# A norm in halves at both ends of a two-layer encoder kernel, and its buffers moved to multiples of 512 bytes

## The reference, cut to what matters

```python
def rmsnorm(x, g):
    y = x * lax.rsqrt(jnp.mean(x * x, axis=-1, keepdims=True) + EPS)
    return y * g

def reference(...):
    for l in range(DEPTH):                    # DEPTH = 2
        hn = rmsnorm(h, mix_pre[l])
        mix = rglru_mixer(hn, ...)  if l == 0 else  swa_sink_attention(hn, ...)
        h = h + rmsnorm(mix, mix_post[l])
        f = swiglu(rmsnorm(h, ffn_pre[l]), ffn_w_gu[l], ffn_w_down[l])
        h = h + rmsnorm(f, ffn_post[l])
    return h
```

## Time and profile before

| | |
|---|---|
| runs, us | 1172.42, 1173.07, 1174.63 (median 1173.07) |
| profiled execution, us | 1173.57; span from the first to the last instruction 1171.6 |
| PE, matmul | 1140.4 us busy, 97% |
| DVE, ACT, POOL | 550.7 (47%), 451.9 (39%), 89.6 us (8%) |
| DMA | 106.98 MB, mean 91 GB/s |
| mean granted TensorE clock | 0.996 |

### The profile page before, as it was taken

How to read it: one execution, slowest core, us unless ns; L and a number is a source line. 1 busy time by engine, 2 the same in 40 slices (tenths; PEclk the granted TensorE clock), 3 DMA queues, 4 the chain that set the end, 5 groups by cost and what they waited for, 6 DMA issues and landing times.

```text
span 1171.6 us, 13468 instructions
## 1 busy us (share of the span) xinstructions
PE 1140.4 (97%) x5605; PEld 950.9 (81%) x5605; DVE 550.7 (47%) x688; ACT 451.9 (39%) x715; POOL 89.6 (8%) x73
## 2 busy tenths in 40 slices
PE   7999998999999999999999899999999999999997
PEld 6888887889888888888888878788888888888885
DVE  4868977756333333322237577446433333332224
ACT  5365565445223222221116467545323232221112
POOL 1003213200000000000012332100000000000000
PEclk9999999999999999999999999999999999999999
DMA  6241333213433333332332421122433333332311
GB/s 192 79 112 46 90 101 108 90 54 109 126 106 93 92 106 90 102 96 90 92 88 58 123 55 37 37 72 84 134 107 90 98 100 90 106 92 90 97 46 72
DMA packets 150798, 106.98 MB, mean 91 GB/s; under 512 B 23905, under 2 KB 140753, under 8 KB 150738
## 3 DMA queue, kind: packets, MB, share of 16 engines
q1 hardware_dynamic: 150402, 106.06, 31.2%
q10 hardware_dynamic: 336, 0.07, 0.0%
HBM read 104.01 MB, written 2.10 MB: 91 GB/s over the span
## 4 chain that ended last, share of the span: by engine, by line
PE 77%; DVE 14%; ACT 6%; issue 1%; POOL 1%; ACTq 0%; PEldq 0%; POOLq 0%
PE ps L1091 15%; PE ps L1092 15%; PE ps L1093 15%; PE ps L1110 9%; PE ps L1111 9%; PE ps L1114 9%; DVE xc L869 2%; DVE w_lo L757 1%; PE ps L1120 1%; ACT w_hi L475 1%; DVE t_i L855 1%; ACT s_sb L687 1%; ACT junk L479 1%; DVE work L919 1%; DVE xc_lo L878 1%
## 5 line engine op out<-in xcount | busy, mean ns | idle before, releaser
L757 DVE TENSOR_TENSOR w_lo<-raw,w_hi 128x1024 fp32r<-128x1024 f32 x176 | 220.5, 1253 | 512.0 <-ACT w_hi L475 512.0
L1091 PE MATMUL ps<-x_hi,w_hi 128*128 128x512 f32 (+1 forms) x1096 | 405.8, 370 | 7.0 <-DVE w_lo L757 4.5
L1092 PE MATMUL ps<-x_lo,w_hi 128*128 128x512 f32 (+1 forms) x1096 | 402.8, 368 | 0.0
L1093 PE MATMUL ps<-x_hi,w_lo 128*128 128x512 f32 (+1 forms) x1096 | 402.7, 367 | 0.0
L475 ACT CAST w_hi<-raw 128x1024 fp32r<-128x1024 f32 x186 | 195.1, 1049 | 434.4 <-PE ps L1093 251.7
L1091 PEld LDWEIGHTS ps<-x_hi,w_hi 128*128 128x128 f32 x1096 | 208.1, 190 | 43.5 <-DVE w_lo L757 6.4
L1093 PEld LDWEIGHTS ps<-x_hi,w_lo 128*128 128x128 f32 x1096 | 208.1, 190 | 33.4
L1092 PEld LDWEIGHTS ps<-x_lo,w_hi 128*128 128x128 f32 x1096 | 208.2, 190 | 32.9
L1110 PE MATMUL ps<-w_hi,hid 128*128 128x512 f32 x352 | 139.2, 395 | 0.0
L1111 PE MATMUL ps<-w_lo,hid 128*128 128x512 f32 x352 | 139.0, 395 | 0.0
L1114 PE MATMUL ps<-w_hi,hid 128*128 128x512 f32 x352 | 110.3, 395 | 0.0
(11 more groups left out here) (144 smaller groups left out, 1056.6 us busy)
## 6 DMA issues: line engine op xcount, KB each, us to landing
raw<-in_ffn_w_gu SPq DMA_DIRECT2D x88, 512.0 KB, 3.8
raw<-in_ffn_w_down SPq DMA_DIRECT2D x44, 512.0 KB, 3.6
raw<-in_a_w_in SPq DMA_DIRECT2D x24, 512.0 KB, 4.1
raw<-in_a_w_out SPq DMA_DIRECT2D x12, 512.0 KB, 3.5
raw<-in_b_w_q SPq DMA_DIRECT2D x16, 256.0 KB, 3.6
raw<-in_b_w_o SPq DMA_DIRECT2D x16, 256.0 KB, 3.8
h<-in_x SPq DMA_DIRECT2D x4, 512.0 KB, 5.8
result<-h SPq DMA_DIRECT2D x4, 512.0 KB, 2.6
```

What stands on the lines that cost most here:

```text
L757: v.tensor_tensor(w_lo[:, t % 4, :], raw[:, t % 4, :], w_hi[:, t % 4, :].bitcast(F32), ALU.subtract)\
L1091: nc.tensor.matmul(out_ps, hi_w, hi_x, start=first, stop=False)
L1092: nc.tensor.matmul(out_ps, hi_w, lo_x, start=False, stop=False)
L1093: return nc.tensor.matmul(out_ps, lo_w, hi_x, start=False, stop=final)
```

## The change

There are four edits. In the first tiles, `START_PARTS` cuts tiles 0 and 1 into two halves of 512 features: norm, transposes, `x_hi` and `x_lo` go half by half, and the first products take four of the eight slices of 128 features as soon as those are there. POOL takes the subtraction of weight tile 0 from DVE. The eight parameter DMAs go from ACT's queue to SP's, behind the loads of weight tiles 1 to 3, and in their place ACT takes one root of a constant (`eps`) before x is there. In the last token tile, PE finishes the first 512 result columns before it begins the last steps of the other 512; squares, the product with the gain, the addition and the write go by these halves, and the product with the gain comes ahead of the reciprocal. Last, the first buffer and the region of the stage buffers are rounded up to a multiple of 512: the first group of buffers goes from 16512 to 16896, the stage buffers from 138240 to 138752. With that both groups begin at multiples of 512.

```diff
+START_PARTS = [(0, 0, 4), (0, 4, 8), (1, 0, 4), (1, 4, 8), (2, 0, 8), (3, 0, 8)]
...
-    at = {"top": (nc.sbuf_base + 63) // 64 * 64}
+    at = {"top": (nc.sbuf_base + 511) // 512 * 512}
...
+    at["top"] += -at["top"] % 512
     U = at["top"]
...
+            for half in range(2):
+                sp.wait_ge(h_ready, 4 * TC + half)
+                cols = slice(half * S, half * S + S)
+                sp.dma_start(out[0, S - P:S, cols], h[:, TC - 1, cols]).then_inc(out_stored, 16)
...
+            pool.wait_ge(w_hi_ready, 1)
+            nc.gpsimd.tensor_tensor(w_lo[:, 0, :], raw[:, 0, :], w_hi[:, 0, :].bitcast(F32), ALU.subtract)\
+                .then_inc(w_lo_ready, 1)
...
+            act.wait_ge(eps_ready, 1)
+            nc.scalar.activation(std[:, 32:33], eps[:, 0:1], ACT.Sqrt)
...
+            for half in range(2):
+                act.wait_ge(last_acc, half + 1)
+                nc.scalar.activation(junk[:, 0:S], bank(2 * TC - 2 + half), ACT.Square, scale=D ** -0.5,
+                                     accum_out=last_ss[:, half:half + 1]).then_inc(last_sq, 1)
+                act.wait_ge(last_sq, half + 1)
+                if half == 0:
+                    nc.scalar.activation(last_ss[:, 2:3], last_ss[:, 0:1], ACT.Identity, bias=eps[:, 0:1])\
+                        .then_inc(last_sum, 1)
+            act.wait_ge(last_sum, 1)
+            n = post_at(3, TC - 1)
+            nc.scalar.activation(std[:, n:n + 1], last_ss[:, 1:2], ACT.Sqrt, bias=last_ss[:, 2:3]).then_inc(std_ready, 1)
...
+            for half in range(2):
+                dve.wait_ge(last_sq, half + 1)
+                cols = slice(half * S, half * S + S)
+                v.tensor_tensor(work[:, 1, cols], bank(2 * TC - 2 + half), gpost[:, cols], ALU.mult)\
+                    .then_inc(last_steps, 1)
+            r = reciprocal(post_at(3, TC - 1))
+            dve.wait_ge(last_steps, 2)
+            for half in range(2):
+                cols = slice(half * S, half * S + S)
+                v.scalar_tensor_tensor(out=h[:, TC - 1, cols], in0=work[:, 1, cols], scalar=r, in1=h[:, TC - 1, cols],
+                                       op0=ALU.mult, op1=ALU.add).then_inc(h_ready, 1)
...
+            def first_half(i):
+                tile_ready(i)
+                for part in range(2):
+                    pe.wait_ge(first_lo, 3 + part)
+                    columns(i, i, range(4 * part, 4 * part + 4), slice(0, S // 2))
+
+            for i in range(4):
+                first_turn(i)
+            first_half(0)
```

More of the change, by code:

```diff
@@ L734, in _ @@
             split_hi(T_END - 1)
-            for t in range(TC):
+            for t in range(TC - 1):
                 post(3, t)
+            for half in range(2):
[9 more added lines that the diff above has]
+            nc.scalar.activation(std[:, n:n + 1], last_ss[:, 1:2], ACT.Sqrt, bias=last_ss[:, 2:3]).then_inc(std_ready, 1)
         @block.vector
@@ L769, in x_low, with normalise_x, first_low @@
                     .then_inc(xlo_ready, 1)
-            def normalise_x(t):
-                r = reciprocal(pre_at(-1, t))
-                if t == 0:
+            def normalise_x(i):
+                t, k0, k1 = START_PARTS[i]
+                n = pre_at(-1, t)
+                r = reciprocal(n) if k0 == 0 else rstd[:, n:n + 1]
+                if i == 0:
                     dve.wait_ge(gain_spread, 1)
                 if t >= 2:
[L777 to L786, removed]
+                    dve.wait_ge(first_turned, 2 * t - 2)
+                cols = slice(k0 * P, k1 * P)
+                v.scalar_tensor_tensor(out=work[:, t % 2, cols], in0=h[:, t, cols], scalar=r, in1=acc(3)[:, cols],
+                                       op0=ALU.mult, op1=ALU.mult).then_inc(first_hn, 1)
+            def first_low(i):
+                t, k0, k1 = START_PARTS[i]
+                dve.wait_ge(first_hi, i + 1)
+                tok = slice(t * P, (t + 1) * P)
+                v.tensor_tensor(x_lo[:, k0:k1, tok], turned_in(t)[:, k0:k1, :], x_hi[:, k0:k1, tok].bitcast(F32),
+                                ALU.subtract).then_inc(first_lo, 1)
+            for i in range(4):
+                normalise_x(i)
+            for i in range(4):
+                first_low(i)
+            normalise_x(4)
             split_lo(1)
-            normalise_x(3)
-            x_low(-1, 2)
+            normalise_x(5)
+            first_low(4)
             split_lo(2)
-            x_low(-1, 3)
+            first_low(5)
             dve.wait_ge(rows_ready, 1)
@@ L1127, in token_half @@
                     tile_ready(t)
-                pe.wait_ge(xlo_ready, TC * (b + 1) + 2 * half + 2)
+                pe.wait_ge(xlo_ready, TC * b + 2 * half + 2)
                 ins = columns(t, i, tok=slice(half * S // 2, (half + 1) * S // 2))
@@ L1167, in boundary @@
                     drain(b, 2, range(k0, n_tiles), *args)
-                    drain(b, 3, range(k0, n_tiles), *args)
+                    for half in range(2):
+                        tok = slice(S - P, S)
+                        for k in range(k0, n_tiles):
+                            ins = rows(first_tile + k, TC - 1, hi(k)[:, tok], lo(k)[:, tok], False, k == n_tiles - 1,
+                                       (half,))
+                        ins.then_inc(last_acc, 1)
                     return
@@ L1193, in _, with first_turn @@
             ins.then_inc(gain_spread, 1)
[L1194 to L1200, removed]
+            def first_turn(i):
+                t, k0, k1 = START_PARTS[i]
+                pe.wait_ge(first_hn, i + 1)
+                for k in range(k0, k1):
+                    ins = nc.tensor.transpose(turned_in(t)[:, k, :], work[:, t % 2, k * P:(k + 1) * P], ident[:, :])
+                ins.then_inc(first_turned, 1)
+            def first_half(i):
[3 more added lines that the diff above has]
+                    columns(i, i, range(4 * part, 4 * part + 4), slice(0, S // 2))
+            for i in range(4):
+                first_turn(i)
+            first_half(0)
+            first_turn(4)
+            first_half(1)
+            first_turn(5)
+            first_half(2)
             pe.wait_ge(params_landed, 16 * 8)
             nc.tensor.transpose(ps[:, 3, 0:R_ROWS], r_rows[0:R_ROWS, :], ident[0:R_ROWS, 0:R_ROWS]).then_inc(rows_ready, 1)
+            pe.wait_ge(first_lo, 6)
             for i in range(3):
-                token_half(-1, i, 0, 1)
+                columns(i, i, tok=slice(S // 2, S)).then_inc(tiles_done, 1)
             def gate_bank_free(n, g):
```

59 lines of the change are left out of this document (38 added, 21 removed).

## The result

The changed kernel takes 1159.05 us (median, 1157.66 to 1159.49, 4 runs) against 1173.51 (1172.42 to 1174.63, 4 runs) for the one before. The ratio is 0.9877, 95% interval 0.9863 to 0.9892: faster by 14.5 us. The forecast was 1158.0. The profiled execution took 1159.33, its span is 1157.4, so 14.2 less than before.

The account below looks back on a forecast made before the run. PE bounds the kernel, with matmuls in flight 97% of the span. Start -4.4, end -1.9 and placement -9.0 sum to -15.3 from 1173.57: 1158.3, about 1158 with the 0.5 to the median; range 1155.5 to 1168.5.

Parts of the forecast that it names:

- Start, -4.4: Before the first product: shorter chain from x's landing, first product at about 11.6 instead of 16.06; bounds -2.5 to -6.5.
- End, -1.9: After the last matmul: earlier root, halved instructions behind the reciprocal, smaller last write; bounds -1.3 to -2.6 us.
- Placement, -9.0: In `rows` and the gates: equal remainders modulo 512 bring 512-column products to 0.2262 us; 8.4 plus half of 1.2.
- in stages where PE waits for nobody: Claim about the 1536 `rows` products: their faster pace, worth 8.4 us, is gained where PE has no waits.
- The rule behind it: Placement's premise: pace depends on operand offsets modulo 512; equal remainders give 0.2262 us against 0.2317 and 0.2331.
- The rival built on it: Placement does nothing; the 0.2317 pace belongs to the region from 138240 or something else that stays: 1166.8 us, chance 0.34.
- zero is bad: Full pace needs neither operand at a multiple of 512, so `columns` slows, price +14.1: about 1181 us, chance 0.08.
- Start pinned: Late weights, POOL's subtraction or DVE's parameter chain leave 2.5 of the start's 4.4 us, pace gained: 1160 us, chance 0.08.

Follow-up runs that it names:

- `x_hi` apart: Changed kernel with h, `x_hi` and `x_lo` 128 bytes past a multiple of 512, all other buffers at multiples: 1170.86 us, ratio 0.9975.
- The experiment with ACT's order: Changed kernel with the last recurrent group's three tanh of the first gate ahead of the rounding of y chunk 8 on ACT: 1154.46 us, ratio 0.9838.
- Equal at 128: Changed kernel with both groups of buffers 128 bytes past a multiple of 512: 1160.03 us, ratio 0.9882.
- 256 apart: Changed kernel with the stage buffers 256 bytes past a multiple of 512, first group at zero: 1158.03 us beside 1175.39 for the kernel before.
- the last experiment on ACT's order: Kernel before, with only the three tanh moved ahead of the rounding of y chunk 8 on ACT: 1169.48 us beside 1173.45, ratio 0.9966.
- placement alone: Kernel before with only the two roundings of buffer starts to 512 bytes: 1167.29 us beside 1173.57, ratio 0.9937.
- 64 and 32 apart: Two runs: changed kernel with the stage buffers 64 or 32 bytes past a multiple of 512, first group at zero: 1170.28 and 1170.39 us.

## Why the prediction was right

**Start, -4.4, measured -4.5.** The chain came nearly step by step: root from 5.89 (6.1 to 6.4 forecast), halves of 0.70, the last transposes until 10.9 (10.6), POOL from 8.65 to 11.01 (9.1 to 11.5, since the weight tile landed in 5.5 and not 6.0), first product at 11.53 (11.6). POOL took 2.36, no more than in the earlier trace rows. One statement failed without a consequence: the parameter DMAs were to be issued by 8.5, but they were issued only from 10.0 on, as the issue of weight tiles 1 to 3 kept SP until 9.95; they were still in time. And the forecast that the first 24 products all stay at the lower clock was somewhat too careful: 20 did where all 24 had before. That is part of the 0.8 that came behind the start.

**End, -1.9, measured -2.0.** All three steps hold: root 0.5 earlier relative to the last matmul (0.43 forecast), two halved instructions behind the reciprocal, write 2.0.

**Placement, -9.0, net measured about -7.7; with the old places beside it, -9.3.** The table's seven stretches between first product and last matmul make -7.7 together before rounding, and some of that is the clock at the start. The comparison that has nothing but placement in it is the changed kernel against the same with old places: 9.6 us by the medians, 9.3 by the spans (1166.7 and 1157.4). So the size of the term was right, by contributions that were not all right. The two feed-forward parts gave 2.9 and 3.0 us, and 528 products x 0.0055 is 2.9. The stretch of the gates gave 1.1, all of 168 x 0.0069, where half was counted. What failed is "in stages where PE waits for nobody": it doesn't hold for the output projection of the first mixer, whose row has the 3.3 us wait. There 288 products were to give 1.6 us, and the wait took back 0.8 of them. It stood in the rows, and it should have been asked who ends it: a chain of DVE and POOL that no faster matmul moves.

**What the sum had no term for** is the fall of the clock behind that wait, some 1.6 to 1.8 us. It came with the old places too, so in these traces it is not a price of placement. Of the twelve traces with the old order in ACT's queue ten have it; the two without are the kernel before and the one with `x_hi` apart, whose wait was 1.7. The experiment with ACT's order shows what wait and clock cost together: the changed kernel gives 4.6 more.

**The rule behind it** was half right. The theory spoke of the remainder modulo 512, with two cases (0 and 128 apart). Equal at 128 confirmed the equality, the moved `x_hi` confirmed that it is the pair; 256 apart refuted the 512, which the prediction took from the steps of 512 bytes in which `columns` walks its weights.

The Trainium skill (SBUF — State Buffer, "SBUF: two separate sides") says that PE never waits on anyone at its SBUF ports, from which the prediction drew that placement would be worth nothing. The experiments disagree with that: the same program is 9.6 us slower with the old places, with 518 matmuls against 531 in the same stage and clock. The rival built on it forecast 1166.8; the kernel with the old places, which is what it describes, took 1168.65; the rival's sum lacks the fall of the clock as well.

**The rival "zero is bad"** fell with `columns` at 884, and with both at 128 taking about the same time as both at 0. **"Start pinned"** fell with 11.53. That the forecast of 1158 was hit to 1.05 us was partly luck. In the fourth stretch 1.6 us were to be won and 0.8 were lost, 2.4 too few; 0.8 from the clock behind the start and 0.5 in the gates, neither of them counted, made up for half of that.

**What stays open.** Why 256 bytes: the runs show the period, not its cause. What decides the fall of the clock: over the fourteen traces the length of the idle stretch ahead of it does not. Each trace is one execution, and executions differ: in the nine of the kernel before that were taken beside the last experiment on ACT's order, the mean clock went from 0.991 to 0.997 and the time from 1172.1 to 1175.5. At the output projection the clock fell behind all seven waits of 4.1 to 4.2 us (for 3.4 us in four traces, for 6.8 in three), behind one of 3.7, and behind 3.3 in two traces of three; it stayed up behind 1.7, 1.6 and 0.7. In the scores PE waits 3.6 us in every trace, before and after, and the clock fell every time, for 6.8 us but for one trace with 3.4. And near 740 us it fell for 3.4 us in four traces (placement alone, `x_hi` apart, 64 and 32 apart) behind idle stretches of 0.6 and 0.8 us, which the other ten traces have as well. Last, what 1.3 of the 4.0 us are that the reordering gave the kernel before: the stretch that was edited shows 2.7, and 1.1 is the clock at the start in one execution.

## What to carry to other kernels

Two matmuls of one instruction, one width and one clock that come at different intervals are worth a look at where their two operands lie; count matmuls per window, since a busy share of 100% shows nothing of it. A gain in pace is paid out only up to the next wait that another engine ends, so for each stage that gets faster ask which chain ends its wait, and look in the queue of that engine for work that stands ahead of it and has no hurry. When PE starts earlier, part of it can go to the clock: compare a later milestone as well as the first matmul, and several executions. And before a shortfall is put down to one edit, run the kernel with everything but that edit: here the fall of the clock looked like a price of placement, and came without it.

## What the runs showed of the hardware

- By the windows, a 512-column product of fp32r operands comes every 0.2262 us (884 in 200) when the byte offsets of stationary and streamed operand are equal modulo 256 (both at 0, both at 128, or 0 and 256), and every 0.2317 to 0.2328 us (518 and 517 in 120, 859 in 200) when they are 32, 64 or 128 apart, the distances tried. Here that is 9.6 us (`rows` and gates) or 11.8 (`columns`) of 1160.
- Behind idle stretches of 4.1 to 4.2 us in mid-kernel the granted clock was 0.50 for 3.4 us or for 6.8 us: 9 matmuls in 3.4 us in the changed kernel, 11 in 6.8 with placement alone. Behind the same wait of 3.3 us it stayed at 1.00 in the kernel before and was 0.50 for 3.4 us with the old places.
- In one execution a start 2.3 us later cost only 0.5 us at the gates, because the clock stood at its upper level when the products began; over four executions it cost 1.85 in the median.
- One ACT table load ahead of the data served square, root and rounding: the second load of 1.28 us is gone from the chain.
